# Two chained transformer blocks on one core: loads, copies, first groups and adaLN sums reordered, and one GpSimd subtraction of 1024 columns per weight unit

## The chip, the cores and the metric

The kernel runs on one core of a Trainium2 chip. The metric is device time in microseconds (us) of one execution of the whole program. The weights stream from HBM; no input is resident.

## The reference

Two blocks follow each other on 256 tokens of width 1024, all in fp32. The first is a two-layer decoder, the second a two-layer network whose layers are modulated by an adaLN vector. Cut to what matters:

```
# first block, for l in 0, 1
h = rmsnorm(x, g_mix_pre[l]);  parts = split(h @ w_in[l])          # 1024 x 1952
mix = concat(diff_attention, mla_attention, swa_attention) @ w_out[l]
x = x + rmsnorm(mix, g_mix_post[l])
xo = softmax(q(x) @ k(mem)) @ v(mem) @ w_xo[l]                      # w_xq, w_xkv, w_xo
x = x + rmsnorm(xo, g_x_post[l])
gate, up = split(rmsnorm(x, g_ffn_pre[l]) @ w_ffn_in[l])            # 1024 x 5632
x = x + rmsnorm((silu(gate) * up) @ w_ffn_out[l], g_ffn_post[l])    # 2816 x 1024
# second block: mod = silu(c) @ ada_w + ada_b gives shift, scale, gate (9 vectors a layer);
# y = swiglu_ffn(x * (1 + scale) + shift); x = layer_norm(ALPHA * x + res * gate * y)
# context and x pass a half-step FFN; layer 0: FFN, neighbourhood attention, FFN;
# layer 1: FFN, short convolution (sc_w_in, sc_conv, sc_w_out), FFN
```

## The kernel before

**Tiling.** The 256 tokens are two tiles of 128 (`t` = 0, 1). Every big product keeps the activations (128x128 pieces, transposed) as TensorE's stationary operand and streams weights as the moving one. Weights arrive in 654 units of 128x1024 fp32 through a ring of four slots. A product in fp32 accuracy is made of three matmuls on fp32r operands: `w_hi*h_hi`, `w_lo*h_hi`, `w_hi*h_lo` (L2138 to L2140). So a unit passes four engines: SyncE (SP) issues its DMA into `land` (L621) when the slot's last low half is made; ScalarE (ACT) rounds it to `w_hi` (L892, `split`) when TensorE has used the slot's last unit; GpSimd (POOL) makes `w_lo = land - w_hi` (L787, `lo`), in two operations of 512 columns; TensorE (PE) runs 12 matmuls of 512 columns on it.

**Groups.** A group is four units: the whole contraction of 1024 for 512 output columns. `group` (L2149 on) goes by unit: both token tiles of a unit, 12 matmuls, then the next unit. `group_by_tile` goes through all four units for tile 0 (6 matmuls each), then again for tile 1; it frees the first slot only after 30 matmuls. It opens the products whose input `h` is still being made. `first_group(width, aside)` is the first group of an FFN or of the K and V product of the neighbourhood attention; with `aside` (set at two places: the first FFN of layer 0 of the second block, and that K and V product) the input `h` was made earlier, and the output goes to banks TURN and OUT.

**FFN.** `ffn_in` is 11 groups, `ffn_out` 22 units, each with four parts (2 tiles x 2 halves of 512 columns, 3 matmuls a part). The last four units are taken apart: tile 0's halves first, so that the norm of tile 0 runs while PE does tile 1. `then` puts the making of the next `h` (transposes, L2506) ahead of these four.

**AdaLN.** The modulation (two layers of 18 groups of 512 columns) is summed beside the rest: SP loads `ada_land` in four pieces a group (`ada_begin`; a piece waits until DVE has used the last group's piece), VectorE (DVE) sums 8 steps for each vector (`ada_sums`, L2048 and L2051; two vectors in groups 0 to 9, then one) and splits the sum in high and low (L2057, L2060), PE adds over the partitions (`ada_sum`, L2739 and L2740), DVE adds the bias (`ada_rows_out`, L2071). Where PE does it inside an `ffn_out` is set by tables: after unit 7, 12 and 17 (`ADA_OUTS`), or 7 and 13 (`ADA_OUTS_2`); loads of a group start at the unit two less.

**Order.** Each engine has its own program, in program order; all of them are written from one list of stages (`forward`), and semaphores tie them. There is no scheduler. Names of stages used below: in0, mixer0, xq0, xo0, ffn_in0, ffn_out0 and the same with 1 for the first block; F200 for the context's FFN; F0a, NA, F01, F10, conv, F11 for the second.

The lines that the text refers to: L469 to L514 (`forward`), L567 to L700 (SP), L780 to L790 (`lo`), L905 to L985 (ACT at the start), L1133 on (`make_h`), L1612 (`products_q` on DVE), L2036 on (`ada_sums`), L2164 to L2204 (PE's groups), L2434 on (`ffn_out`).

## Time and profile before

| | us |
|---|---|
| median of three runs (2251.19 to 2258.12) | 2252.46 |
| the profiled execution, its own time | 2254.71 |
| its span, first to last instruction | 2252.8 |
| PE busy | 2154.2 (96%) |
| POOL busy | 1686.8 (75%) |
| ACT busy | 1070.5 (48%) |
| DVE busy | 966.1 (43%) |
| mean granted TensorE clock | 0.991 |

The profiled execution took 1.9 us more than its span, the time before the first and after the last instruction. Matmuls are pipelined, so the busy time of PE counts overlapping matmuls once, and a busy PE need not run at its full rate. L-numbers are lines of the kernel before. PEld is TensorE's weight load, POOL is GpSimd, SPq and ACTq are DMA issues of SyncE and ScalarE.

### The profile page before, as it was taken

Reading aid. Unit: us, or ns where it says so; the run is one execution under the profiler, and the core shown is the slowest. Engines: PE = TensorE matmul, PEld = TensorE weight load, DVE = VectorE, ACT = ScalarE, POOL = GpSimd, SP = SyncE. Lnnn points to the kernel's source line nnn. Section 1 sums busy time; section 2 is a strip of 40 time slices with the busy share of each in tenths; the row PEclk is TensorE's granted clock in tenths of the full one; section 3 lists DMA queues with packets and bytes.
Section 4 is the critical chain, followed back from the end, with each engine's and each line's share of the span. In section 5 each row is a group of like instructions: output and inputs, shape, how many; then the busy total and the mean of one; then the engine's idle time right before and its main releaser. Section 6 shows DMA issues by size and latency. Waiting matters only on the chain.

```text
span 2252.8 us, 32261 instructions
## 1 busy us (share of the span) xinstructions
PE 2154.2 (96%) x10197; PEld 1741.4 (77%) x10197; DVE 966.1 (43%) x1892; ACT 1070.5 (48%) x1646; POOL 1686.8 (75%) x1361
## 2 busy tenths in 40 slices
PE   8998899999988999999999999999999999999997
PEld 6787778778877787788778877887887788687886
DVE  6355676753556544544543552364111310344112
ACT  4464444445653544444454454565444544435442
POOL 5646388877544888798888879726988888697986
PEclk9999999999999999999999999999999999999999
DMA  7535387755244786687878765523656566464663
GB/s 232 165 113 163 103 296 257 261 182 166 92 138 179 260 284 255 211 300 244 296 255 284 282 218 162 187 76 113 203 179 198 166 186 207 139 222 145 193 205 120
DMA packets 135863, 447.10 MB, mean 198 GB/s; under 512 B 22539, under 2 KB 28131, under 8 KB 135769
## 3 DMA queue, kind: packets, MB, share of 16 engines
q1 hardware_dynamic: 129080, 426.62, 57.4%
q10 hardware_dynamic: 6688, 19.23, 2.5%
q8 instruction: 58, 0.95, 0.2%
q14 instruction: 37, 0.30, 0.0%
HBM read 444.60 MB, written 3.03 MB: 199 GB/s over the span
## 4 chain that ended last, share of the span: by engine, by line
POOL 49%; issue 29%; PE 20%; DVE 1%; POOLq 1%; ACT 0%; DMA 0%; SPq 0%; ACTq 0%; DVEq 0%
POOL w_lo L787 48%; PE ps L2138 5%; PE ps L2140 5%; PE ps L2139 5%; PE ps L2647 1%; PE ps L2612 1%; PE ps L2635 1%; PE ps L2475 1%; POOLq L187 0%; PE ps L2608 0%; POOL ada_land L833 0%; POOLq L785 0%; PE ps L2578 0%; PE ps L2390 0%; PE ps L2580 0%
## 5 line engine op out<-in xcount | busy, mean ns | idle before, releaser
L787 POOL TENSOR_TENSOR w_lo<-land,w_hi 128x512 fp32r<-128x512 f32 x1300 | 1650.3, 1303 | 518.0 <-ACT w_hi L892 516.9
L892 ACT ACTIVATE w_hi<-land 128x1024 fp32r<-128x1024 f32 x654 | 692.5, 1061 | 942.4 <-PE ps L2140 736.9
L2138 PE MATMUL ps<-w_hi,h_hi 128*128 128x512 f32 (+1 forms) x1840 | 734.6, 399 | 52.8 <-POOL w_lo L787 24.4
L2140 PE MATMUL ps<-w_hi,h_lo 128*128 128x512 f32 (+1 forms) x1840 | 720.6, 392 | 0.0
L2139 PE MATMUL ps<-w_lo,h_hi 128*128 128x512 f32 (+1 forms) x1840 | 719.5, 391 | 0.0
L2138 PEld LDWEIGHTS ps<-w_hi,h_hi 128*128 128x128 f32 x1840 | 348.0, 189 | 150.1 <-POOL w_lo L787 39.6
L2140 PEld LDWEIGHTS ps<-w_hi,h_lo 128*128 128x128 f32 x1840 | 347.8, 189 | 74.0
L2139 PEld LDWEIGHTS ps<-w_lo,h_hi 128*128 128x128 f32 x1840 | 348.4, 189 | 67.3
L1530 DVE TENSOR_TENSOR hid_lo<-ps,hid_hi 128x512 f32 (+1 forms) x77 | 53.2, 691 | 550.5 <-ACT hid_hi L1044 550.5
L2138 PE MATMUL ps<-w_hi,hid_hi 128*128 128x512 f32 x616 | 245.2, 398 | 5.7 <-POOL w_lo L787 5.7
L2140 PE MATMUL ps<-w_hi,hid_lo 128*128 128x512 f32 x616 | 243.5, 395 | 0.0
L2139 PE MATMUL ps<-w_lo,hid_hi 128*128 128x512 f32 x616 | 243.4, 395 | 0.0
L2051 DVE SCALAR_TENSOR_TENSOR ps<-ada_land,ccol,ps 128x512 f32<-128x512 f32 x322 | 230.5, 750 | 20.6 <-DMA ada_land<-ada_w_dram 12.6
L2138 PEld LDWEIGHTS ps<-w_hi,hid_hi 128*128 128x128 f32 x616 | 115.7, 188 | 36.5 <-POOL w_lo L787 7.9
L2140 PEld LDWEIGHTS ps<-w_hi,hid_lo 128*128 128x128 f32 x616 | 115.7, 188 | 28.0
L2139 PEld LDWEIGHTS ps<-w_lo,hid_hi 128*128 128x128 f32 x616 | 115.8, 188 | 27.0
L1128 ACT ACTIVATE h_hi<-ps 128x512 fp32r<-128x512 f32 x56 | 33.0, 597 | 61.6 <-DVE ps L1479 33.1
L2138 PE MATMUL ps<-w_hi,m_hi 128*128 128x512 f32 x128 | 53.6, 418 | 5.1 <-POOL w_lo L787 3.6
L1647 DVE TENSOR_TENSOR hid<-ps,sg 128x256 f32<-128x256 f32 x110 | 41.1, 415 | 37.8 <-ACT sg L1038 37.8
L1727 DVE SCALAR_TENSOR_TENSOR ps<-ps,rows 128x512 f32<-128x512 f32 x24 | 15.9, 693 | 93.2 <-PE ps L2140 93.2
L2140 PE MATMUL ps<-w_hi,m_lo 128*128 128x512 f32 x128 | 51.2, 400 | 0.0
L2139 PE MATMUL ps<-w_lo,m_hi 128*128 128x512 f32 x128 | 51.2, 400 | 0.0
(276 smaller groups left out, 1911.4 us busy)
## 6 DMA issues: line engine op xcount, KB each, us to landing
land<-ffn_w_in_dram SPq DMA_DIRECT2D x220, 512.0 KB, 3.6
ada_land<-ada_w_dram SPq DMA_DIRECT2D x144, 512.0 KB, 5.2
land<-ffn_w_out_dram SPq DMA_DIRECT2D x110, 512.0 KB, 4.1
land<-w_ffn_in_dram SPq DMA_DIRECT2D x88, 512.0 KB, 3.9
land<-w_ffn_out_dram SPq DMA_DIRECT2D x44, 512.0 KB, 4.1
land<-na_w_qkv_dram SPq DMA_DIRECT2D x40, 512.0 KB, 4.2
land<-w_xkv_dram SPq DMA_DIRECT2D x32, 512.0 KB, 3.6
land<-w_in_dram SPq DMA_DIRECT2D x32, 488.0 KB, 3.5
```

What stands on the lines that cost most here:

```text
L787: done = pool.tensor_tensor(w_lo[:, slot, half], land[:, slot, half], w_hi[:, slot, half].bitcast(F32), ALU.subtract)
L892: act.activation(w_hi[:, slot, :], land[:, slot, :], ACT.Copy).then_inc(*my.up("hi_ready"))
L1128: act.activation(half_of(h_hi, i), turned_bank(i), ACT.Copy).then_inc(*my.up("split_hi"))
L1530: dve.tensor_tensor(lo_dst, bank(TURN + kp).rearrange("p (a b) -> p a b", a=2), hi_src.bitcast(F32), ALU.subtract).then_inc(*my.up("split_ ...
L1647: ins_ = dve.tensor_tensor(hid[:, g % 2, t, :], got, sg[:, t, :], ALU.mult)
L2051: ins_ = dve.scalar_tensor_tensor(acc, w, c, acc, ALU.mult, ALU.add)
L2138: pe.matmul(dst, lh, wh, start=first, stop=False)
L2139: pe.matmul(dst, lh, wl, start=False, stop=False)
L2140: done = pe.matmul(dst, ll, wh, start=False, stop=last)
L2475: done = pe.transpose(ps[0:m, b, c * SEQ + t * P:c * SEQ + (t + 1) * P], tile, ident[:, :])
L2612: yield pe.matmul(s[:, t * SEQ:(t + 1) * SEQ], q[:, t * P:(t + 1) * P], k, start=(c == 0), stop=(c == len(mp["qk"]) - 1))
L2635: done = pe.transpose(ps[:, TURN + m % 2, at * P:(at + 1) * P], e[:, j * P:(j + 1) * P], ident[:, :])
```

## The change

1. **POOL.** The low half of a unit is one operation of 1024 columns in place of two of 512.
2. **Start.** The eight small tables (`load_constants`) are issued by SP behind the first four weight units, no longer by ACT; ACT makes the first high half of `h` ahead of the first unit's, issues the load of `mem` last, and splits `tables` in two: it rounds four units, squares `mem` (`square_memory`), rounds one unit, runs `tables`, rounds three.
3. **K and V weights of layer 0.** The seven DMAs that shift the position bias in DRAM stand behind units 7 to 13 of this stream instead of ahead of it.
4. **`aside` groups** go by unit (`group`) and not by tile.
5. **Last four units of `ffn_out`.** Tile 0's parts go in the order of `LAST_FOUR`: both halves of units 0 and 1, the first halves of 2 and 3, the second halves of 2 and 3.
6. **AdaLN.** In `ffn_out` PE adds after units 8, 13, 17 (ffn_out0), 8, 13 (ffn_out1) or 8, 12, 16 (F200, F0a), and loads start three units before. In `products_q` DVE makes four of the eight steps, copies out the first half of the queries, and then makes the rest. In `products_y` the second product's sum is added on PE one unit later, and the second of two loads starts at unit 5, its last steps behind the last unit.

```diff
-ADA_OUTS, ADA_OUTS_2, COLUMNS_AT = (7, 12, 17), (7, 13), 9
+ADA_OUTS, ADA_OUTS_2, ADA_OUTS_3, COLUMNS_AT = (8, 13, 17), (8, 13), (8, 12, 16), 9
...
+LAST_FOUR = ((0, 0), (0, 1), (1, 0), (1, 1), (2, 0), (3, 0), (2, 1), (3, 1))
...
+RPB_AT = 7
...
-            do("ffn_out", "ffn_w_out_200", ada=ADA_OUTS, then=dict(src="x", mod=(0, 0)))
+            do("ffn_out", "ffn_w_out_200", ada=ADA_OUTS_3, then=dict(src="x", mod=(0, 0)))
...
+            def products_in(l):
+                stream(f"w_in{l}", 0, 16, None if l else {RING - 1: load_constants})
...
             def kv_weights(w):
                 if n_kv[0] == 0:
-                    for j in range(7):
-                        src = bass.AP(ins["na_rpb_2"].tensor, (4 + j) * RPB_W + 15,
-                                      [(RPB_H * RPB_W, NA_H), (-1, GRID), (1, GRID)])
-                        sp.dma_start(rpb_w[:, :, j, :], src).then_inc(sems["rpb_out"], 16)
-                stream(w, 0, KV_UNITS)
+                    stream(w, 0, KV_UNITS, {RPB_AT + j: lambda j=j: shifted_rpb(j) for j in range(7)}, rolled=False)
+                else:
+                    stream(w, 0, KV_UNITS)
...
-                extra = ada_extra([3] if keys else [0, 3][0:sums])
+                extra = ada_extra([3] if keys else [0, 5][0:sums])
+                if sums > 1:
+                    late = [extra.pop(at) for at in (8, 9)]
+                    extra[7] = lambda steps=[extra[7], *late]: [step() for step in steps]
...
-                extra = ada_extra([at - 2 for at in ada])
+                extra = ada_extra([at - 3 for at in ada])
...
-                for half in (slice(0, UW // 2), slice(UW // 2, UW)):
-                    done = pool.tensor_tensor(w_lo[:, slot, half], land[:, slot, half], w_hi[:, slot, half].bitcast(F32), ALU.subtract)
-                done.then_inc(*my.up("lo_ready"))
+                pool.tensor_tensor(w_lo[:, slot, :], land[:, slot, :], w_hi[:, slot, :].bitcast(F32), ALU.subtract).then_inc(*my.up("lo_ready"))
...
                 if l == 0:
+                    split(RING)
+                    square_memory()
+                    split(1)
+                    tables()
                     split(RING - 1)
-                    tables()
-                    split(RING + 1)
...
                 if now:
+                    high(0)
                     split(1)
-                    high(0)
                     high(1)
                     split(RING - 1)
-                    load_constants()
                     high(2)
                     high(3)
+                    load_io("mem")
                     return
...
             def products_q(w):
                 dve.wait_ge(*my.last())
-                ada_sums()
+                ada_steps(range(0, KC // 2))
                 scaled_out("q_x", 0, GW, 0, R_X, "taken")
-                dve.wait_ge(*my.last())
+                ada_sums(range(KC // 2, KC))
                 ada_rows_out()
...
-                group_by_tile((TURN, OUT) if aside else (0, 2), width, fresh=True, aside=aside)
-                if aside:
+                if not aside:
+                    group_by_tile((0, 2), width, fresh=True)
+                else:
+                    pe.wait_ge(sems["split_lo"], my.at("split_lo", n["split_lo"]))
+                    group((TURN, OUT), width)
...
                 if sums:
-                    after[2] = ada_sum
+                    after[3] = ada_sum
...
-                for half in range(2):
-                    for j in range(4):
-                        if half == 0:
-                            pe.wait_ge(sems["lo_ready"], my.at("lo_ready", u + j + 1))
-                        done = part(u + j, FC - 4 + j, {0: (half,)})
-                    done.then_inc(*my.up("y_ready"))
+                for j, half in LAST_FOUR:
+                    if half == 0:
+                        pe.wait_ge(sems["lo_ready"], my.at("lo_ready", u + j + 1))
+                    done = part(u + j, FC - 4 + j, {0: (half,)})
+                    if j == 3:
+                        done.then_inc(*my.up("y_ready"))
```

Two places of the order, before and after the change (line numbers of the change are higher by 14 to 26).

ScalarE in in0, from the fifth weight unit on. Before: `L892` rounds a unit, `L927` squares `mem`, `L929` to `L933` are the tables.

```order
L892 ACTIVATE w_hi<-land 128x1024 [waits w_used,landed2]
L927 ACTIVATE z,stat<-io 128x1024 [waits io_in,squares]
L927 ACTIVATE z,stat<-io 128x1024
L929 ACTIVATE csig<-ccol 128x16 [waits start_in]
L931 ACTIVATE lam<-lam 128x4 [waits start_v]
L932 ACT_TABLE_LOAD
L932 ACTIVATE cosb<-ang 128x32
L933 ACTIVATE sinb<-ang 128x32
L892 ACTIVATE w_hi<-land 128x1024 [waits w_used,landed3]
```

Now:

```order
L918 ACTIVATE w_hi<-land 128x1024 [waits w_used,landed3]
L937 ACTIVATE z,stat<-io 128x1024 [waits io_in,squares]
L937 ACTIVATE z,stat<-io 128x1024
L918 ACTIVATE w_hi<-land 128x1024 [waits w_used,landed0]
L941 ACTIVATE csig<-ccol 128x16 [waits start_in]
L943 ACTIVATE lam<-lam 128x4 [waits start_v]
L944 ACT_TABLE_LOAD
L944 ACTIVATE cosb<-ang 128x32
L945 ACTIVATE sinb<-ang 128x32
L918 ACTIVATE w_hi<-land 128x1024 [waits w_used,landed1]
```

Two units (the eighth in slot 3 and the ninth in slot 0) moved ahead of the tables.

VectorE in xq0, between the row statistics of x and the attention: the adaLN steps and the copies of the queries (`tok_x`). Before:

```order
L2048 TENSOR_SCALAR ps<-ada_land,ccol 128x512 x2
L2051 SCALAR_TENSOR_TENSOR ps<-ada_land,ccol,ps 128x512 x14
L2057 CAST ada_hi<-ps 128x512 x2
L2060 TENSOR_TENSOR ada_lo<-ps,ada_hi 128x512 x2
L1556 TENSOR_SCALAR tok_x<-ps,stat 128x512 x2
L2071 TENSOR_TENSOR ada_o<-ps,ada_b 2x512
L1556 TENSOR_SCALAR tok_x<-ps,stat 128x512 x2
```

Now:

```order
L2061 TENSOR_SCALAR ps<-ada_land,ccol 128x512 x2
L2064 SCALAR_TENSOR_TENSOR ps<-ada_land,ccol,ps 128x512 x6
L1570 TENSOR_SCALAR tok_x<-ps,stat 128x512 x2
L2064 SCALAR_TENSOR_TENSOR ps<-ada_land,ccol,ps 128x512 x8
L2076 CAST ada_hi<-ps 128x512 x2
L2079 TENSOR_TENSOR ada_lo<-ps,ada_hi 128x512 x2
L2090 TENSOR_TENSOR ada_o<-ps,ada_b 2x512
L1570 TENSOR_SCALAR tok_x<-ps,stat 128x512 x2
```

The first copy of the queries moved ahead of eight steps and of the split of the sum, which now stand behind it.

## Rows read from the trace of the kernel before

**Rows 1.** The page: busy time, share of the span and instructions of each engine.

```profile
PE 2154.2 (96%) x10197; PEld 1741.4 (77%) x10197; DVE 966.1 (43%) x1892; ACT 1070.5 (48%) x1646; POOL 1686.8 (75%) x1361
```

**Rows 2.** Waits by pair: engine, line, waited for: total us, times, longest.

```profile
PEld ps L2138 <- POOL w_lo L787: 51.8, 51, 5.1
```

**Rows 3.** Timeline in F200: start us, us, engine, operation [idle before].

```profile
1001.50 0.39 PE L2138 MATMUL ps<-w_hi,h_hi 128*128 128x512 f32 x1
1001.73 0.39 PE L2139 MATMUL ps<-w_lo,h_hi 128*128 128x512 f32 x1
...
1002.16 2.55 POOL L787 TENSOR_TENSOR w_lo<-land,w_hi 128x512 fp32r<-128x512 f32 x2 [0.17 <-ACT w_hi L892]
```

**Rows 4.** POOL: groups by form; and timeline, eight operations behind each other.

```profile
L855 POOL TENSOR_TENSOR x<-z,rows 128x1024 f32<-128x1024 f32 x1 | 2.3, 2347 | 10.0 <-ACT z L1233 10.0
...
932.04 10.00 POOL L787 TENSOR_TENSOR w_lo<-land,w_hi 128x512 fp32r<-128x512 f32 x8 [6.46 <-ACT w_hi L892]
```

**Rows 5.** Timeline of PE at the last four units of F01.

```profile
1732.77 0.50 PE L2138 MATMUL ps<-w_hi,hid_hi 128*128 128x512 f32 x1 [1.69 <-POOL w_lo L787]
```

**Rows 6.** Timeline of PE, sixth unit of F10 behind a layer norm.

```profile
1771.29 0.50 PE L2138 MATMUL ps<-w_hi,h_hi 128*128 128x512 f32 x1 [0.46 <-POOL w_lo L787]
```

**Rows 7.** Timeline of PE and ACT, first group of F0a.

```profile
1133.98 0.50 PE L2138 MATMUL ps<-w_hi,h_hi 128*128 128x512 f32 x1 [1.24 <-POOL w_lo L787]
...
1138.94 0.49 PE L2138 MATMUL ps<-w_hi,h_hi 128*128 128x512 f32 x1 [0.81 <-POOL w_lo L787]
...
1138.95 1.21 ACT L1209 ACTIVATE z<-ps,stat 128x1024 f32<-128x1024 f32 x1
```

**Rows 8.** Timeline of SP and ACT at the K and V product of NA.

```profile
1319.20 15.88 SPq L723 DMA_DIRECT2D ada_land<-rpb_w  x24
1335.44 14.32 SPq L621 DMA_DIRECT2D land<-na_w_qkv_dram  x7
...
1339.59 1.06 ACT L892 ACTIVATE w_hi<-land 128x1024 fp32r<-128x1024 f32 x1 [2.30 <-DMA land<-na_w_qkv_dram]
```

**Rows 9.** Timeline of PE, waits at the adaLN sums of ffn_out0, ffn_out1 and F200.

```profile
437.09 0.40 PE L2739 MATMUL ps<-ada_hi,pick_r 128*2 128x512 f32 x1 [1.22 <-DVE ada_lo L2060]
...
892.55 0.39 PE L2739 MATMUL ps<-ada_hi,pick_r 128*2 128x512 f32 x1 [1.08 <-DVE ada_lo L2060]
...
1118.21 1.94 PE L2506 MATMUL ps<-ident,x 128*128 128x128 f32 x16 [1.07 <-DVE ada_o L2071]
```

**Rows 10.** Timeline of DVE, two ends of sums in ffn_out0.

```profile
438.22 0.68 DVE L2071 TENSOR_TENSOR ada_o<-ps,ada_b 2x512 f32<-2x512 f32 x1 [1.18 <-PE ps L2740]
...
453.32 0.68 DVE L2071 TENSOR_TENSOR ada_o<-ps,ada_b 2x512 f32<-2x512 f32 x1 [1.18 <-PE ps L2740]
```

**Rows 11.** Timeline of DVE and PE in xq0.

```profile
213.85 9.31 DVE L2051 SCALAR_TENSOR_TENSOR ps<-ada_land,ccol,ps 128x512 f32<-128x512 f32 x14
225.72 1.40 DVE L1556 TENSOR_SCALAR tok_x<-ps,stat 128x512 f32<-128x512 f32 x2
...
227.17 1.97 PE L2475 MATMUL ps<-ident,tok_x 128*128 128x128 f32 x8 [4.93 <-DVE tok_x L1556]
...
233.97 2.32 PE L2612 MATMUL ps<-keysT,qT_x 128*128 128x256 f32 x10
```

**Rows 12.** Timeline of PE at the start, and a stretch with its clock: us, PE busy (x), PEclk, DMA share, GB/s.

```profile
37.99 0.78 PE L2138 MATMUL ps<-w_hi,h_hi 128*128 128x488 f32 x1 [4.65 <-POOL w_lo L787]
...
38.00:42.50 4.50, 4.50 (x11) 0.50 0.58 148
```

**Rows 13.** Timeline of DVE in in0 (distances), and the group of L1805 by form.

```profile
40.56 2.60 DVE L1441 TENSOR_SCALAR dist<-pos_r,pos_c 128x256 f32<-128x256 f32 x2
...
L1805 DVE TENSOR_TENSOR ps<-z,rows 128x1024 f32<-128x1024 f32 x10 | 20.7, 2066 | 0.7
```

**Rows 14.** Timeline of ACT and PE: first K and V unit of layer 0.

```profile
67.27 1.06 ACT L892 ACTIVATE w_hi<-land 128x1024 fp32r<-128x1024 f32 x1 [9.96 <-DMA land<-w_xkv_dram]
...
70.94 0.50 PE L2138 MATMUL ps<-w_hi,m_hi 128*128 128x512 f32 x1 [3.60 <-POOL w_lo L787]
```

More of the change, by code:

```diff
@@ L489, in forward @@
                 ln_rows(i, 0, 2, 0)
-                do("ffn_out", f"ffn_w_out_2{i}0", ada=ADA_OUTS if i == 0 else (), then=dict(src="z", folded=0) if i == 0 else None)
+                do("ffn_out", f"ffn_w_out_2{i}0", ada=ADA_OUTS_3 if i == 0 else (), then=dict(src="z", folded=0) if i == 0 else None)
                 do("ln", "x", 0.5, FC, folded=None if i == 0 else 4)
@@ L765, in _ @@
             forward({
-                "start": start, "products": products, "products_conv": products_conv, "products_in": lambda l: stream(f"w_in{l}", 0, 16), "kv_weights": kv_weights,
+                "start": start, "products": products, "products_conv": products_conv, "products_in": products_in, "kv_weights": kv_weights,
                 "products_q": lambda w: stream(w, 0, 8), "products_na": lambda: stream("na_w_qkv", 0, 4 * NA_GROUPS), "products_y": products_y, "ffn_in": ffn_in, "ffn_out": ffn_out,
@@ L905, in split, with square_memory @@
                     unit()
[L907 to L923 removed]
+            def square_memory():
                 act.wait_ge(sems["squares"], my.at("squares", n["squares"]))
@@ L927, in tables @@
                     act.activation(z[:, t, :], io[:, t, :], ACT.Square, accum_out=stat[:, 28 + t:29 + t]).then_inc(*my.up("squares"))
+            def tables():
                 act.wait_ge(sems["start_in"], my.next("start_in", 16 * START_LOADS))
@@ L2034, in products_conv, with ada_steps @@
                 evict(5)
-            def ada_sums():
-                g = ada_at[0]
-                both = ada_vectors(g)
-                for k in range(KC):
+            def ada_steps(ks):
+                both = ada_vectors(ada_at[0])
+                for k in ks:
                     if k % 2 == 0:
@@ L2052, in ada_sums @@
                         ins_.then_inc(*my.up("ada_steps"))
+            def ada_sums(ks=range(KC)):
+                g = ada_at[0]
+                both = ada_vectors(g)
+                ada_steps(ks)
                 if g > 0:
@@ L2162, in group, with group_by_tile @@
                         after[j]()
-            def group_by_tile(banks, width, fresh=False, after=None, aside=False, left=(h_hi, h_lo)):
+            def group_by_tile(banks, width, fresh=False, after=None, left=(h_hi, h_lo)):
                 u = n["units"]
@@ L2169, in group_by_tile @@
                 for t in range(T):
-                    if fresh and not aside:
+                    if fresh:
                         name, value = free[t]
```

34 lines of the change are left out of this document (18 added, 16 removed).

## The prediction

> **What bounds the kernel now.** I read the page first: PE is busy for 96% of the span and the next engine, POOL, for 75% [rows 1]. In F200's steady state POOL's pair of operations takes 2.55 us and then waits 0.17 us for ScalarE, a cycle of 2.72 us; PE starts its 512-column matmuls 0.23 us apart, and 12 of them fill that same cycle [rows 3]. So PE sets the pace and POOL stands just under it, at 94%. 654 units of 2.72 us are 1779 us that no part of this change touches: its matmuls are the same. What can go is time in which PE waits. The waits by pair put 51.8 us in 51 waits on `w_lo` [rows 2], and the timelines of PE show the rest one by one, on adaLN sums and on copies. A matmul shown behind an idle stretch began about 0.17 us later than the idle says (the row gives the one before it 0.39 us, but the next could start after 0.23), so a wait costs its idle plus 0.17.
>
> **POOL's operation.** The trace has POOL operations of 1024 columns: 2.35 us [rows 4]. Against a pair at 2.55 us on time that is 0.20 less before a low half is ready; eight pairs behind each other take 10.00 us for four units, 2.50 each [rows 4], so in a backlog a unit gains 0.15. Steady stretches gain nothing, PE hides it; when PE's sequence is behind a norm, POOL works through a backlog and PE waits a little at each unit, as at F10's sixth unit, 0.46 + 0.17 [rows 6]. Such waits over the first units of F01, F10, conv and F11 add up to 3.4 us; a backlog of four to six units at 0.15 takes off 0.5 to 0.6 at each: **2.1**. Ten places where single low halves come last (the by-tile first groups of F200 and NA, and the first units of ffn_in0, xq0, ffn_in1, xq1) at 0.12 to 0.20: **1.5**. Bounds for both: 0, if the 1024-column form costs 2.50 here, and 5.
>
> **Last four units.** In F01 PE waits 1.69 + 0.17 = 1.86 at the fourth of them [rows 5], after three parts of 0.68 us (three matmuls) each; F10 and F11 have the same wait. The new order puts two more parts ahead of it, 1.36, and POOL is 0.2 quicker at the most: the wait falls to about 0.48. 3 x 1.38 = **4.1**. Bounds: 3 and 5.6 (all of it gone).
>
> **`aside` groups.** F0a's group waits 1.24 + 0.17 and 0.81 + 0.17 at its units [rows 7], and 0.98 a third time, 3.4 in all; a unit now carries 12 matmuls before the next is needed, so these go. But ScalarE's rounding of the fifth unit stands behind the normalisation of tile 1, which ends at 1140.16 [rows 7]; rounding and low half take some 3.4 more, and a PE that is 3.4 earlier meets it: a new wait of about 1.5. **2.0**. In NA the waits were 3.4 and, on a sum, 1.2; but there SP issues 24 small bias loads over 15.88 us and only then the next weight, at 1335.44; it lands and is rounded at 1339.59 [rows 8], its low half ends at about 1343.1, while PE asked for it at 1343.4. Whatever PE gains ahead, it loses at that unit: **0**, bounds -1.5 and +1.5.
>
> **AdaLN in `ffn_out`.** PE waits for the split sum 1.22 us in ffn_out0, 1.08 in ffn_out1, and 1.07 at the transposes after it in F200 [rows 9], each + 0.17. One unit more (2.72) covers all three: 1.25 in ffn_out1, 1.23 in F200. In ffn_out0 DVE's sums are a chain: two sums end 15.1 us apart [rows 10], and three groups at 8, 13, 17 now leave 9 units, 24.5 us, between the first and the third, for 30.2 us of chain, less what the earlier load gives. The first wait goes (1.39), the third comes in with 2 us or so: **-0.5**, bounds -3 and +1.4. Sum of the three: **2.0**.
>
> **xq0 and xq1.** Fourteen of the sixteen steps take 9.31 us, 0.665 each, and PE's transposes wait 4.93 + 0.17 for the first copy of the queries behind them and the split [rows 11]. With eight steps (5.3) and the split (2.6) moved behind it, the copy is 7.9 earlier and the transposes start at 222.1, when PE is free. DVE does the same operations in another order, so its last one, now the split of the sum instead of the copy, still ends at 227.1. PE, which has done a unit by then (2.7 and the transposes), waits for it some 1.5, adds it up in four matmuls (0.9) and starts the scores at about 228.3, where it did at 233.97 [rows 11]; the stretch at half clock behind the 4.93 us idle is gone with it. **5.7**, bounds 3 (if the new idle brings the half clock too) and 6.4 (no new wait). xq1 has no such wait: 0.
>
> **xo0 and xo1.** PE's waits on the sums go, but DVE's own chain (steps, split, new x) sets when x is ready. I take one wait of the size of ffn_out1's [rows 9] for both together: **1.3**, bounds 0 and 4 (three such).
>
> **Start.** The position bias no longer stands ahead of the K and V weights: ScalarE's 9.96 us wait for the first of them becomes short, and PE's 3.60 + 0.17 goes [rows 14], with a half-clock stretch behind it (1.4): 5.2. In in0 two units are rounded ahead of the tables, and PE's wait of 4.65 + 0.17, which was followed by 4.5 us at a granted clock of 0.50 [rows 12], and another of 0.8 on `h_lo` could go too, in all 9. Against this stands DVE. [...] With POOL's at 2.35 us, each `dist` in lockstep takes 2.35: eight of them, 10.4 us before, take 18.8, and DVE's tile of the queries comes at about 55.4 where PE wants it at 49.8. This takes the 9 back: in0 gets -1.7 in my sum. Start: **3.5**, bounds 0 and 14.
>
> [...]
>
> **Sum.** 2.1 + 1.5 + 4.1 + 2.0 + 0 + 2.0 + 5.7 + 1.3 + 3.5 = 22.2 us. The profiled execution took 2254.7 us, 1.9 beyond its span, and was 2.2 above the median; from it 2254.7 - 22.2 = 2232.5, and by the median 2252.46 - 22.2 = **2230**.
>
> **The rivals.**
>
> *The start keeps its gain* (0.17). DVE's operations there don't stretch with POOL's: then 9 + 5.2 at the start, and 1 more elsewhere, sum 33 and about 2220. For it: it is not shown that a wider POOL operation is one block; against: `dist`'s time equals POOL's operation, not its own size.
>
> *Blocking spreads* (0.15). The mixer's softmax and xq0 also have such DVE operations beside POOL; 16 of them at 0.6 us more, on a path on which PE waits, cost up to 10, and the start and xq0 lose 2. Gain 10: about 2242. For it: same engines, same buffers; against: POOL is idle in much of the mixers, since weights are rounded ahead only as far as the ring of four.
>
> *The change doesn't do what it says* (0.05): one operation of 1024 costs the pair's 2.50. Then 2.1 + 1.5 and part of the last-four term are lost, 4.2: about 2234. The 2.35 us of two other forms [rows 4] speak against it.
>
> *Slower* (0.03). [...]
>
> **How the numbers follow.** The forecast has 0.60, with its own range from 2224 to 2238 by the bounds of its terms (not all fall on one side). 0.3% is 6.8 us, about what a measurement of this kernel can tell from no change; the boundary is 2245.7. The range 2216 to 2244 takes in the first three rivals and leaves out the tails and the slower one. Faster 0.92; within 0.3% 0.06 (the far end of the spreading rival); slower 0.02.
>
> **What would show it.** In the profile after: `w_lo` x650 at 2.35 us mean; F01, F10, F11 with under 0.6 us of wait in the last four; no waits inside F0a's first group, but one at its fifth unit; NA's same unit at the same distance from SP's last bias load; PE's transposes of `tok_x` without a wait, the scores 5.7 us earlier; no 9.96 us wait of ScalarE at the first K and V unit; `dist` at 2.35 us and PE waiting for `scaled_out`'s tile near 50 us. The prediction is wrong if `dist` stays at 1.3, if mixers grow by more than 1 us each, or if steady stretches of `ffn_in` no longer run at 2.72 us per unit, since everything rests on PE's pace being untouched.

## The result, and the profile after it

The changed kernel took 2231.86 us, median of 4 runs (2229.97 to 2238.67), beside 2255.29 us for the kernel before in the same comparison: a ratio of 0.9899, 95% interval 0.9865 to 0.9933. The prediction was 2230 (2216 to 2244). The profiled execution took 2231.26 us, its span 2229.5, against 2254.71 and 2252.8 before.

The total came out within 2 us of the forecast, but several terms did not come out: errors of opposite sign hid each other. So the total is no test of the terms; the stretches of PE are.

First the page of the changed kernel, which answers to [rows 1], and its costliest group on POOL:

```profile
PE 2145.7 (96%) x10197; PEld 1743.3 (78%) x10197; DVE 988.1 (44%) x1892; ACT 1070.1 (48%) x1646; POOL 1594.6 (72%) x711
...
L814 POOL TENSOR_TENSOR w_lo<-land,w_hi 128x1024 fp32r<-128x1024 f32 x650 | 1558.1, 2413 | 580.8 <-ACT w_hi L918 578.2
```

650 operations of 2.41 us stand for 1300 of 1.30; in steady state one takes 2.40, in a backlog they start 2.36 apart. DVE has the same 1892 instructions and is busy 22 us longer. The waits on `w_lo` by pair answer to [rows 2], 51.8 us in 51:

```profile
PEld ps L2157 <- POOL w_lo L814: 13.3, 18, 1.7
PE ps L2157 <- POOL w_lo L814: 13.3, 14, 5.5
```

The table gives the length of stretches of PE, in us, from one stage's first matmul to the next's, worked out from the starts in each trace. The program is the same in a column and the "again" beside it: the kernel before and the changed one were each profiled twice (the second executions are experiments 11 and 12). "Wide alone" is experiment 2, "narrow" experiment 1.

| stretch | before | again | wide alone | narrow | changed | again |
|---|---|---|---|---|---|---|
| in0 | 69.50 | 66.53 | 63.72 | 60.52 | 61.18 | 67.15 |
| K/V and mixer, layer 0 | 95.64 | 95.43 | 96.03 | 93.76 | 95.15 | 95.06 |
| K/V and mixer, layer 1 | 93.03 | 92.58 | 94.33 | 93.19 | 95.92 | 95.52 |
| xq0 | 52.04 | 51.81 | 51.55 | 47.92 | 47.42 | 46.93 |
| xo0 | 28.82 | 28.81 | 28.78 | 28.35 | 28.35 | 28.37 |
| xo1 | 34.04 | 34.15 | 33.22 | 32.02 | 32.02 | 32.00 |
| ffn_out0 | 70.28 | 70.28 | 70.14 | 70.79 | 70.79 | 70.80 |
| F200, ffn_out | 66.41 | 66.40 | 66.41 | 65.14 | 65.14 | 65.14 |
| F0a, ffn_in | 130.71 | 130.72 | 130.15 | 128.38 | 128.25 | 128.23 |
| F0a, ffn_out | 66.40 | 66.40 | 66.41 | 65.14 | 65.14 | 65.14 |
| NA, K and V product | 51.39 | 51.09 | 50.29 | 54.83 | 53.35 | 52.92 |
| NA, the rest | 139.86 | 141.40 | 140.74 | 139.85 | 145.53 | 139.13 |
| F10, ffn_in | 128.73 | 128.71 | 127.38 | 128.70 | 127.36 | 127.38 |
| F10, ffn_out | 70.01 | 70.00 | 69.87 | 68.65 | 68.51 | 68.50 |

The F rows, xo0 and ffn_out0 repeat within 0.1 us from one execution of a program to the next; the mixers, xq0, xo1 and NA's K and V product within 0.5. In0 and NA's rest do not: the second execution of the changed kernel took 6 us more in one and 6 us less in the other, and the sum of all stretches hardly moved, 2215.48 and 2216.11. Some stretches that are not in the table vary too: ffn_in1 took 128.97 and 130.39 us in the changed kernel (the second had 3.1 us at half clock, a granted clock of 0.50), and in the kernel before layer 1's w_in took 49.00 and 47.89 and xq1 45.23 and 46.09.

The places that the prediction named, on PE of the changed kernel. The fourth of the last four units: no stall in F01, F10 or F11 above 0.4 us, where [rows 5] showed 1.69; the row below is F11's. F0a's fifth unit; NA's fifth unit; the third sum of ffn_out0; the sum in xq0, and the scores behind it:

```profile
2209.35 0.50 PE L2157 MATMUL ps<-w_hi,hid_hi 128*128 128x512 f32 x1 [0.20 <-POOL w_lo L814]
...
1124.51 0.50 PE L2157 MATMUL ps<-w_hi,h_hi 128*128 128x512 f32 x1 [1.29 <-POOL w_lo L814]
...
1322.07 0.76 PE L2157 MATMUL ps<-w_hi,h_hi 128*128 128x512 f32 x1 [5.51 <-POOL w_lo L814]
...
454.91 0.39 PE L2761 MATMUL ps<-ada_hi,pick_r 128*2 128x512 f32 x1 [2.82 <-DVE ada_lo L2079]
...
218.58 0.40 PE L2761 MATMUL ps<-ada_hi,pick_r 128*2 128x512 f32 x1 [1.37 <-DVE ada_lo L2079]
219.50 2.75 PE L2634 MATMUL ps<-keysT,qT_x 128*128 128x256 f32 x12
```

Each wait is where the prediction put it: 0.2 + 0.17 (0.48 forecast), 1.5 (1.5), 5.7 (3.4 + 1.2 = 4.6, what PE was to gain ahead of it), 3.0 (2 or so), 1.5 (1.5).

### The profile page after: what moved, and what is told of

It is laid out like the page before. It is cut to its first block, busy times and chain, and to the rows that moved or that the text cites. A ratio compares the mean times of both kernels' runs of the same rounds, so it can differ in the third digit from the quotient of the medians.

```text
span 2229.5 us, 31551 instructions
## 1 busy us (share of the span) xinstructions
PE 2145.7 (96%) x10197; PEld 1743.3 (78%) x10197; DVE 988.1 (44%) x1892; ACT 1070.1 (48%) x1646; POOL 1594.6 (72%) x711
## 4 chain that ended last, share of the span: by engine, by line
PE 35%; POOL 30%; issue 27%; DVE 7%; ACT 1%; POOLq 1%; DMA 0%; SPq 0%; DVEq 0%; ACTq 0%
POOL w_lo L814 29%; PE ps L2157 9%; PE ps L2159 9%; PE ps L2158 9%; PE ps L2669 2%; DVE ps L2064 1%; PE ps L2657 1%; PE ps L2634 1%; PE ps L2497 1%; PE ps L2630 0%; PE ps L2412 0%; POOLq L191 0%; DVE h_lo L1502 0%; POOL ada_land L859 0%; POOLq L813 0%
## 5 line engine op out<-in xcount | busy, mean ns | idle before, releaser
L814 POOL TENSOR_TENSOR w_lo<-land,w_hi 128x1024 fp32r<-128x1024 f32 x650 | 1558.1, 2413 | 580.8 <-ACT w_hi L918 578.2
```

What stands on the lines that cost most here:

```text
L814: pool.tensor_tensor(w_lo[:, slot, :], land[:, slot, :], w_hi[:, slot, :].bitcast(F32), ALU.subtract).then_inc(*my.up("lo_ready"))
```

## The experiments

Times are spans and medians as given by each run; the verdicts rest on stretches of PE, since one execution of this kernel differs from the next by several us. Where a run has one execution only, the text says so. In the short diffs `-` is the changed kernel unless said otherwise.

### 1. Narrow: two operations again

```diff
-                pool.tensor_tensor(w_lo[:, slot, :], land[:, slot, :], ...)
+                for half in (slice(0, UW // 2), slice(UW // 2, UW)):
+                    done = pool.tensor_tensor(w_lo[:, slot, half], land[:, slot, half], ...)
```

> The change with POOL's one operation of 1024 columns put back to two of 512; everything else as changed. Theory A (the wide operation ends a low half 0.15 to 0.2 us sooner, but blocks an operation of DVE on the shared path for its whole length, as L1877 in mixer0, 0.27 us before and 1.21 after): in each of the two mixers PE's waits behind the probabilities go back from 1.64 and 2.71 to 0.89 and 1.77, 1.7 us a layer, 3.4 in all; at the start DVE's operations on the angles (2.33 us each) halve and PE's 3.83 us wait for zin falls under 1, 4 us; the latencies give back 3.6 to 4. Net 3 to 5 us shorter than the change, 2225 to 2229. Theory B (the wide operation costs DVE nothing that reaches PE): mixers and start unchanged, 3.6 us longer than the change, 2235.

2231.9 us median of 4, ratio to before 0.9887 (0.9857 to 0.9917): no difference from the change that the medians can show. In the stretches A holds for the mixers, 1.4 and 2.7 us shorter, and for the low halves, 1.3 us longer in F10's and F11's ffn_in, 0.6 in F01's, conv's and F200's. It fails for the start: in0 changed by 0.7, not 4. The gain and the price of the wide operation stand in different places. Over the stretches from F200 on, NA's attention left out, the wide operation is 7.0 us shorter by the two profiles; the mixers cost 3.4 by their waits (below). A net gain of 3 or 4 us is less than the intervals of the two medians can tell from nothing.

### 2. Wide alone, in the kernel before

```diff
 (kernel before)
-                for half in (slice(0, UW // 2), slice(UW // 2, UW)):
-                    done = pool.tensor_tensor(w_lo[:, slot, half], land[:, slot, half], ...)
-                done.then_inc(*my.up("lo_ready"))
+                pool.tensor_tensor(w_lo[:, slot, :], land[:, slot, :], ...).then_inc(*my.up("lo_ready"))
```

> The kernel before with the one operation of 1024 columns alone. Theory A: 3.6 us gained at the low halves (last four of ffn_out: each wait 1.86 to about 1.65; by-tile groups 0.12 to 0.2 each; sixth units of F10, conv, F11 0.3 each), 3.4 us lost in the mixers, and a loss of some us in in0, where eight DVE operations go from 1.3 to 2.35 each; net 0 to 8 us longer than before. Theory B: 3.6 us shorter than before, no stretch longer.

2246.09 us median of 10, ratio 0.9955 (0.9934 to 0.9975): faster by about 10 us (5.6 to 14.9), more than either theory said, and more than its stretches that repeat show. Those behind norms gave 4.4 us: F01 0.70, F10 1.35, conv 0.59, its second product 0.36, F11 1.39. The mixer of layer 1 lost 1.3 (1.8 against the second execution of before). In0, which I had expected to lose, was 63.72, less than in either execution of before. The cause is not the low half alone: PE did not wait for the first K and V unit there, which it does in both executions of before (3.77 and 3.6 us).

### 3. NA's first group by tile again

```diff
-                    pe.wait_ge(sems["split_lo"], my.at("split_lo", n["split_lo"]))
-                    group((TURN, OUT), width)
+                    n_aside.append(1)
+                    if len(n_aside) == 2:
+                        group_by_tile((TURN, OUT), width, fresh=True, aside=True)
+                    else:
...
```

> The change, but the first group of NA's K and V product goes by tile again. Theory A (SP's 24 bias loads ahead of the fifth unit set when that unit comes, whatever PE gained ahead, and an idle of 5.7 us brings a stretch of PE at half clock that a row of short waits does not): the wait of 5.67 at unit 380 falls to under 1.5, short waits of 0.8 to 1.2 come back at the first three half units, no half clock, and the K and V stretch (53.35 us in the change, 51.39 before) comes out near 51: 2 us shorter. Rival: the stretch depends on the unit alone, so 53.3 again. Whether the half clock in NA's attention (1455 to 1463, 5.5 us lost) comes back is open: it is the same code and the same waits as before.

The K and V product took 51.84 us (53.35 and 52.92 in the change): A, with 1.1 to 1.5 us. The wait at the fifth unit was 1.8, the short waits were 1.25, 0.85 and 0.86. No part of this stretch ran at half clock; 6.8 us of it did in both executions of the change. So the change by unit costs at this place: PE, which is 3.4 us earlier, meets SP's bias loads in one long idle (5.5 us in the change's first profile), and the granted clock is 0.50 for 6.8 us around its end. 2 us had been expected. The median of four was 2229.17 (2222.91 to 2234.54), ratio 0.9878 (0.9841 to 0.9915).

### 4. NA's bias loads spread

```diff
-                for h in range(NA_BIAS):
-                    load_bias(h)
+                for h in range(NA_BIAS):
+                    for r in range(4):
+                        spread_out.append(lambda h=h, r=r: bias_part(h, r))
```

and `stream` issues two of the list behind each unit, from the fifth on.

> The change, with NA's 24 bias loads issued two behind each weight unit of the K and V product from the fifth on, not all ahead of the fifth. Theory A: the 5.67 us wait at unit 380 and the half clock behind it go and the K and V stretch falls from 53.35 to about 45.5, total 7 us shorter than the change, 2224. Rival (the fifth unit is late for another cause, ScalarE's normalisation as in F0a): the wait stays at 1.5 or more, 4 us shorter at most.

47.92 us: 5.2 less than the mean of the change's two. The wait fell from 5.7 to 1.56 and the granted clock was 1.00 all through the stretch. 7 us had been expected, with the stretch near 45.5. What is left at that unit is the rival's cause, as in F0a: ScalarE rounds the unit (from 1318.10 us on) directly behind its normalisation of tile 1. The median was 2225.67 (2222.62 to 2230.55), ratio 0.987 (0.9838 to 0.9903). The change leaves this gain unused.

### 5. Position bias ahead of the K and V weights again

```diff
-                    stream(w, 0, KV_UNITS, {RPB_AT + j: lambda j=j: shifted_rpb(j) for j in range(7)}, rolled=False)
+                    for j in range(7):
+                        shifted_rpb(j)
+                    stream(w, 0, KV_UNITS)
```

> The change, with the seven shifts of the position bias issued ahead of the K and V weights of layer 0 again. Prediction's term: 5.2 us lost (PE idle 3.77 at the first K and V unit and a half-clock stretch). Rival, from the run of the wide operation alone, where the first K and V unit landed 5.9 us after its issue, not 9.4 as before, and PE did not wait: the term depends on how fast these small transfers land in one execution, and PE, which gets to that unit at 62 us and not at 67, waits 2 to 9 us.

In0 61.37 us (61.18) and the stretch behind it 96.79 (95.15): 1.8 us in all, and no wait of PE at the first K and V unit. This is one execution (2233.06 us); in experiment 4, which has the change's code in both stretches, they took 61.27 and 96.09, and beside that it is 0.8. ScalarE waited there, though less than the 9.96 us of [rows 14]:

```profile
59.22 1.06 ACT L920 ACTIVATE w_hi<-land 128x1024 fp32r<-128x1024 f32 x1 [6.31 <-DMA land<-w_xkv_dram]
```

SP issued the seven shifts from 44.38 us on, 5.3 us earlier than before, and PE came to the unit at 62.8, when its low half was just ready. Neither the 5.2 us of my term nor the rival's wait of 2 to 9 us came. The 5.2 was the price in the kernel before; with SP running ahead in the changed kernel, the same DMAs cost 0.8 to 1.8.

### 6. ScalarE's old order in in0

```diff
-                    split(RING)
-                    square_memory()
-                    split(1)
-                    tables()
-                    split(RING - 1)
+                    split(RING - 1)
+                    square_memory()
+                    tables()
+                    split(RING + 1)
```

> The change, with ScalarE's old order in in0 (three units, squares of mem and the tables together, five units). Theory A: the eighth and ninth units' high halves come after the squares and the tables, which now wait for SP's eight tables, and PE's idle at unit 7 comes back: 4 to 5 us, of which 3.8 were at unit 8 for zin in the change, so in0 grows by 1 to 4 us from 61.2 (with a half clock, at the upper end). Rival: mem's load, now last on ScalarE's queue, is there in time and nothing is lost: in0 stays within 0.5 us.

In0 60.86 us, 0.3 less, where 1 to 4 more had been expected: the wait at unit 7 came back (3.14) and the one at unit 8 (3.83) went. One queue or the other makes PE wait about as long there. Rounding two units earlier gave nothing in this one execution (2227.76 us).

### 7. First copy of the queries behind the sum again

```diff
-                ada_steps(range(0, KC // 2))
-                scaled_out("q_x", 0, GW, 0, R_X, "taken")
-                ada_sums(range(KC // 2, KC))
+                ada_sums()
+                scaled_out("q_x", 0, GW, 0, R_X, "taken")
+                dve.wait_ge(*my.last())
```

> The change, with the first copy of xq0's and xq1's queries behind all sixteen steps and the split again. Theory: PE's 5.1 us wait at unit 47 comes back and the waits of 1.53 on the sum and 2.12 behind the second copy go; with the half clock xq0 is 4 to 5 us longer than 47.42, xq1 within 1 us.

Xq0 took 52.07 us, as before (52.04), against 47.42 and 46.93: this edit is worth 4.9 us by itself (one execution, 2238.02 us). Xq1 took 44.49 (44.52). PE's wait is the one of [rows 11] again:

```profile
224.20 1.97 PE L2497 MATMUL ps<-ident,tok_x 128*128 128x128 f32 x8 [4.98 <-DVE tok_x L1570]
```

The change has another wait there, which the prediction did not have: 1.96 us of idle ahead of the scores of tile 1. It is a block like those of experiment 8. Behind the first scores DVE has an operation of two columns, and the operations of the changed kernel, DVE's and POOL's, are:

```profile
222.33 2.03 DVE L1881 TENSOR_SCALAR mstat<-mstat 128x2 f32<-128x2 f32 x1
```

```profile
221.98 2.35 POOL L814 TENSOR_TENSOR w_lo<-land,w_hi 128x1024 fp32r<-128x1024 f32 x1 [2.02 <-ACT w_hi L918]
```

In experiment 6 POOL's operation came about 2 us earlier, and the block and the wait were gone; xq0 took 45.70:

```profile
221.92 0.31 DVE L1880 TENSOR_SCALAR mstat<-mstat 128x2 f32<-128x2 f32 x1
```

```profile
219.86 2.35 POOL L814 TENSOR_TENSOR w_lo<-land,w_hi 128x1024 fp32r<-128x1024 f32 x1 [0.59 <-ACT w_hi L918]
```

In the ten profiles with the changed order, this DVE operation took 0.17 to 2.13 us; in the seven in which it took 0.57 or more, PE's idle was shorter than it by 0.06 or 0.07, and in the other three it was 0.25 or less.

In this execution in0 took 66.83 us, though its code up to there is the change's (see experiment 11).

### 8. Narrow in in0 and the mixers, wide elsewhere

```diff
+                if my.narrow:
+                    for half in (slice(0, UW // 2), slice(UW // 2, UW)):
+                        done = pool.tensor_tensor(w_lo[:, slot, half], land[:, slot, half], ...)
+                    done.then_inc(*my.up("lo_ready"))
+                    return
...
+                my.narrow = my.n["units"] < 34 or 138 <= my.n["units"] < 158
```

> The change, but two operations of 512 columns for units 4 to 33 and 138 to 157 (in0, and layer 1's K and V, with the mixers), one of 1024 elsewhere. Theory A (DVE's small shared-path operations in the mixers wait for the running POOL operation to end, whatever their own size): mixer stretches as in the narrow kernel, 93.8 and 93.2 (1.4 and 2.7 shorter than the change), in0 0.5 shorter, all other stretches as in the change: 4.5 us shorter. Rival B (the mixers' difference was the clock's): no stretch differs by more than 0.5.

2218.2 us median of 4 (2217.63 to 2220.82), ratio 0.9849 (0.9813 to 0.9886). Layer 1's mixer took 92.64 us, 3 us less than the change. Not all of that is the block, for 3.4 us of the change's stretch ran at half clock and none of this one. In the profiles in which none of the stretch did, it took 94.34 with the wide operation (experiment 2) and 92.37 to 92.64 with narrow ones (the second execution of before, this one and experiment 9): 1.7 to 2.0 us. So A holds, and B accounts for the rest.

Layer 0's stretch came out no shorter (95.32, with 4.1 us at half clock against the change's 1.7). It gained at unit 28, whose wait fell to the narrow one's 0.9, but not at the last scores: my limit of 34 ended before the units that POOL subtracts behind its norm of the heads (34 and 35), where layer 1's (158) includes them. So one kernel holds both cases at that place, layer 0's with wide operations first, then layer 1's with halves:

```profile
149.43 2.08 PE L2643 MATMUL ps<-qkT 64*128 64x256 f32 x8 [2.55 <-ACT prob L1304]
...
604.02 1.13 PE L2643 MATMUL ps<-qkT 64*128 64x256 f32 x8 [1.62 <-ACT prob L1304]
```

2.55 as in the change, 1.62 as before. ScalarE's probabilities are what PE waits for; behind them is DVE. In the changed kernel's layer 0, POOL and DVE (L1877 has two columns, 0.23 us where nothing blocks it):

```profile
147.51 4.66 POOL L814 TENSOR_TENSOR w_lo<-land,w_hi 128x1024 fp32r<-128x1024 f32 x2
```

```profile
150.98 1.21 DVE L1877 TENSOR_SCALAR mstat<-mstat,sinks 128x2 f32<-128x2 f32 x1
...
153.55 0.23 DVE L1877 TENSOR_SCALAR mstat<-mstat,sinks 128x2 f32<-128x2 f32 x1
```

POOL's second operation ends at 147.51 + 4.66 = 152.17; the two-column operation that began inside it ends at 152.19. The next one, with POOL idle, takes its own 0.23.

### 9. Quarters in the mixers

```diff
+                    for part in range(my.narrow):
+                        half = slice(part * UW // my.narrow, (part + 1) * UW // my.narrow)
...
+                my.narrow = 2 if my.n["units"] < 16 else 4 if my.n["units"] < 38 or 138 <= my.n["units"] < 158 else 0
```

> The change, with two operations of 512 columns for units 4 to 15, four of 256 columns for units 16 to 37 and 138 to 157, one of 1024 elsewhere. Theory A (a DVE operation on the shared path waits for the one POOL operation that runs, so its length is that operation's): the waits in both mixers, 1.64 and 2.71 in the change, 0.89 and 1.77 with halves, go on falling, to about 0.5 and 1.3; but a unit takes POOL about 2.8 us there. Mixer stretches 0.5 to 1 us shorter than with halves (93.8, 92.6). Rival: the time from 1.64 to 0.89 came from the earlier low half alone, then quarters, whose unit is later still, make the waits longer than with halves.

Mixer stretches 93.25 and 92.37 us (halves in experiment 10: 93.36 and 93.18). The wait at unit 28, 1.64 and 0.89, fell to 0.25, as A says. The one at the last scores, 2.72 and 1.78, did not go on falling: 2.20. There one small operation, which with halves happened to begin just before the end of one of POOL's and took 0.27, now met one at its start:

```profile
144.81 0.70 DVE L1887 TENSOR_SCALAR mstat<-mstat,sinks 128x2 f32<-128x2 f32 x1
```

So the block shrinks with POOL's operation, but where a given small operation meets one is a matter of phase. The stretches gained 0.1 and 0.8 on the halves, where 0.5 to 1 had been expected. Of the 0.8, about 0.6 is the clock: the halves' stretch of layer 1 had 1.2 us at half clock, the quarters' none. The median of four was 2224.86 us (2218.21 to 2229.01), ratio 0.9875 (0.9852 to 0.9898).

### 10. The two gains together

Narrow for units 4 to 37 and 138 to 157 (as in experiment 8, the limit mended), and NA's bias loads spread (experiment 4).

> The change, with two operations of 512 columns for units 4 to 37 and 138 to 157 and the NA bias loads spread two to a unit: the mixers' 4.1 us and NA's K and V product's 5.4 us together, and both kernels beaten: 2215 us, 9 to 17 us below the change by what in0 and the clock happen to do; ratio to before 0.982 to 0.984. If the two gains are not additive (PE meets another wait behind them), 2221.

2218.68 us median of 5 (2213.28 to 2222.37), ratio 0.9835 (0.9813 to 0.9858). Mixers 93.36 and 93.18, K and V product 47.86: both gains are there together, 4.5 and 5.3 us by the stretches. It is faster than the kernel before by 1.65%; beside the change it is 13 us less by the medians, and its interval ends (0.9858) where the change's two begin (0.9865, and 0.9855 in experiment 11). Against experiment 8, in which in0 came out at 56.3, it is no faster (2218.2 there): in0 took 60.96 here, with the same code.

### 11. The changed kernel once more

> The changed kernel as it is, once more. If the half-clock stretch of PE in NA's attention (13.7 us long, 5.7 us lost) and the length of in0 (61.2 us) are the program's, both come back within 0.5 us. If they are one execution's, NA's 24 units and attention come out at 139 to 142 us, as in seven of the eight other kernels with the same NA code, and in0 at 56 to 67, as DVE's small operations fall before or behind POOL's first low half.

2231.91 us in the profiled execution, 2225.25 in the other, ratio 0.9886 (0.9855 to 0.9916). Neither stretch came back: in0 67.15, NA's rest 139.13. In NA the waits are the same in both, the same 1.68 us before the same product, but not the clock. The windows of PE over the same 14 us of NA's attention, which stands 7 us later in the second profile (us, PE busy (x), PEclk, DMA share, GB/s), first profile and then second:

```profile
1453.00:1467.00 14.00, 14.00 (x65) 0.51 0.16 42
```

```profile
1460.00:1474.00 14.00, 14.00 (x118) 1.00 0.27 68
```

In0 is the better find. PE, first profile and second, at the thirteenth unit, waiting for DVE's copy of tile 1:

```profile
51.47 0.48 PE L2157 MATMUL ps<-w_hi,h_hi 128*128 128x488 f32 x1 [0.41 <-DVE zin L1570]
```

```profile
55.50 0.78 PE L2157 MATMUL ps<-w_hi,h_hi 128*128 128x488 f32 x1 [5.80 <-DVE zin L1570]
```

DVE ahead of that copy. First profile:

```profile
43.50 0.18 DVE L1474 TENSOR_TENSOR ccol<-ccol,csig 128x16 f32<-128x16 f32 x1
43.72 0.62 DVE L1455 TENSOR_SCALAR dist<-pos_r,pos_c 128x256 f32<-128x256 f32 x2
44.37 2.85 DVE L1457 SCALAR_TENSOR_TENSOR dist<-dist 128x512 f32<-128x512 f32 x1
47.25 2.77 DVE L1458 TENSOR_TENSOR dist_w<-dist,band 128x512 f32<-128x512 f32 x1
50.06 1.36 DVE L1570 TENSOR_SCALAR zin<-ps,stat 128x488 f32<-128x488 f32 x2
```

Second profile:

```profile
43.67 2.12 DVE L1474 TENSOR_TENSOR ccol<-ccol,csig 128x16 f32<-128x16 f32 x1
45.82 2.70 DVE L1455 TENSOR_SCALAR dist<-pos_r,pos_c 128x256 f32<-128x256 f32 x2
48.56 2.75 DVE L1457 SCALAR_TENSOR_TENSOR dist<-dist 128x512 f32<-128x512 f32 x1
51.34 2.71 DVE L1458 TENSOR_TENSOR dist_w<-dist,band 128x512 f32<-128x512 f32 x1
54.09 1.36 DVE L1570 TENSOR_SCALAR zin<-ps,stat 128x488 f32<-128x488 f32 x2
```

And POOL, first and second:

```profile
36.10 7.05 POOL L814 TENSOR_TENSOR w_lo<-land,w_hi 128x1024 fp32r<-128x1024 f32 x3 [4.51 <-ACT w_hi L918]
44.27 2.40 POOL L814 TENSOR_TENSOR w_lo<-land,w_hi 128x1024 fp32r<-128x1024 f32 x1 [1.11 <-ACT w_hi L918]
```

```profile
36.23 14.52 POOL L814 TENSOR_TENSOR w_lo<-land,w_hi 128x1024 fp32r<-128x1024 f32 x6 [3.61 <-ACT w_hi L918]
```

In the first, POOL had a pause of 1.11 us from 43.15 on, and three DVE operations ran in it at their own length, 0.18 and 0.31 each. In the second POOL had six low halves without a pause, and each of those operations but one lasted until one ended. The difference is 4 us on DVE, 5.4 in PE's wait, and 6 with the clock behind it, which was 0.50 for 6.8 us from 53.0 on.

### 12. The kernel before once more

No edit.

> The kernel before as it is, once more. In its first profile the first K and V unit landed 9.4 us after its issue behind the seven shifts of the position bias and PE waited 3.77 us; with the wide operation alone it landed after 5.9 us and PE did not wait. If that wait is the program's, it comes back within 1 us. If it is one execution's, in0 (69.5 us to the first K and V matmul) is 64 to 67 here. All stretches behind the mixer of layer 0 should be the same within 0.2 us but for half-clock stretches of 1.7 us each.

2250.89 us, one execution. The wait at the first K and V unit came back, 3.6 us, so it is no accident of the first profile; experiment 2, which has the same order of loads, did not have it. In0 was 3 us shorter all the same, 1.7 of it because the half clock at the 4.6 us wait lasted 3.4 us and not 6.8. NA's rest had 3.4 us at half clock, which the first profile had not. The stretches behind norms repeat within 0.05. Xq1 (0.9 longer) and ffn_out1 (0.5) did not keep to the 0.2 that was expected, and neither had any time at half clock.

## Why the prediction was right, and where it was not

**Last four units: right.** 1.36 a place against 1.38, and 0.14 from the wide operation. One place of three gave less. In F11 the end is not PE's: DVE's chain of the final norm starts with the first half of tile 0, which follows the last low half at once in either order, before and in the change:

```profile
2233.16 0.70 DVE L1775 SCALAR_TENSOR_TENSOR ps<-ps,rows 128x512 f32<-128x512 f32 x1 [44.94 <-PE ps L2140]
```

```profile
2210.43 0.70 DVE L1789 SCALAR_TENSOR_TENSOR ps<-ps,rows 128x512 f32<-128x512 f32 x1 [44.84 <-PE ps L2159]
```

From there to the end of the span it is 19.7 and 19.0 us. PE's stretch to its last matmul is 1.5 us shorter, the rest after it 0.8 longer. I had added the three places as if each ended in a matmul.

**Low half: right in kind, mis-sized.** After norms 2.1 was forecast, 4.4 measured. I gave a backlog of four to six units 0.15 each. A unit in a backlog takes 2.36 against 2.50, 0.14 less, and yet the waits of 0.42 and 0.63 at the seventh and eighth unit of F10 are both gone (the second is the one of [rows 6], which is the eighth unit and not the sixth). The by-tile places, 1.5 forecast for ten, gave more too: the wide operation alone (experiment 2, both executions of before beside it) took 0.6 from F200's ffn_in, 0.5 from ffn_in0, 0.3 to 0.5 from xq0 and 0.8 to 1.1 from NA's K and V product.

**`aside`: F0a right, NA wrong by 1.9.** F0a's ffn_in gained 2.5, of which 0.6 by the wide operation (2.0 forecast for the edit; 1.9 measured on top of the wide operation, 2.3 without it). In NA the step "whatever PE gains ahead, it loses at that unit: 0" left out what it loses besides: with one idle of 5.5 us instead of three short ones the granted clock is 0.50 for 6.8 us, 4.7 of them with PE busy. The K and V product got 1.9 longer, outside the bounds of 1.5 either way; experiment 3, by tile, takes 1.1 to 1.5 of it back. The sum's wait that I had booked there as a set-off belongs to F0a's ffn_out, and it went, 1.26, like F200's.

**AdaLN in `ffn_out`: right.** 1.2, 1.3 and -0.5, each as forecast, with the third sum 3.0 us late in ffn_out0.

**xq0: right in mechanism, 0.6 to 1.1 less.** 4.9 by experiment 7, 4.6 to 5.1 by the stretches, for 5.7. The sum's wait was 1.54 as forecast; the step that failed is that nothing else waits. The scores of tile 1 wait (1.96 + 0.17), because DVE's two-column operation behind the first scores is blocked by POOL (experiment 7). Where it was not, with no part of the stretch at half clock (experiments 6 and 9), xq0 took 45.70, a gain of 6.1 to 6.3. So the term depends on when POOL's operation falls. Xo0 and xo1 gave 0.5 and 2.0, for 1.3 forecast for both; before, 3.4 us of xo1 ran at half clock, which the change's first profile did not have.

**Start: the term failed, both ways.** It said 3.5, of 5.2 for the bias shifts and -1.7 for in0. The 5.2 is what a wait cost in the kernel before; in the changed kernel undoing the edit costs 0.8 to 1.8. The -1.7 does not follow from the figures beside it either: 9 gained and a wait of 5.6 leave 3.4, less what the clock takes; and the figures shown for the 9 add up to 7.9 (4.82, half of 4.5, and 0.8). For in0 I took all of DVE's small operations as blocked, one after the other, and so its copy at 55.4. No run shows the term that my sum has for them, eight operations in 18.8 us: from the first of the eight to the end of the last it was 10.5 us in the kernel before, 13.3 in the first profile of the change and 17.2 in the second. What I took for certain is one of two things that happen: the copy ended at 51.4 in the first profile and 55.4 in the second, and PE waited 0.57 and 5.97, for a forecast of 5.6. What I had not seen is that in a pause of POOL's these operations take their own time, 0.18 and 0.31 us where they took 2.12 and 2.44 beside it (experiment 11). Nor had I seen a wait that both profiles have, 3.8 and 3.0 us ahead of the ninth unit, where PE wants DVE's copy for the transposes of `mem`. Which DVE operations meet POOL goes with small shifts. In the six profiles with the change's code in in0, POOL's first low half started between 19.68 and 20.22 us in the four with an in0 of 61.2 to 61.4, and at 20.46 and 20.70 in the two with 66.8 and 67.2. With halves it is the other way round: 19.89 and 20.34 for an in0 of 60.5 and 61.0 (experiments 1 and 10), 20.74 and 20.95 for 56.3 and 56.5 (experiments 8 and 9), with the same code at the start. No run moved that start by itself, so that it decides is argued and not shown.

**Mixers: the rival I gave 0.15 did happen in part.** "Blocking spreads" priced the mixers at up to 10; it was 3.4 by the waits (1.64 for 0.89 and 2.71 for 1.77, in each layer), and my sum had 0. In layer 1 it is visible in the stretch, 2.9 longer, of which 1.7 to 2.0 is the block and the rest the clock (experiment 8). In layer 0 it is hidden: there the kernel before had 6.4 us at half clock, 3.4 of them behind its wait for the first K and V unit, and the changed one 1.7. By the prediction's own sign of being wrong, mixers more than 1 us longer, this part was wrong in layer 1, and by the waits in both; and `dist`, which was to be at 2.35, took 0.31 in the first profile (experiment 11). The rival's step held in xq0 as well. In experiments 8, 9 and 11 a small DVE operation that began beside one of POOL's ended within 0.05 us after it: 1.21 for an operation of 0.23, 2.12 for one of 0.18, and 0.70 for one of 0.23 when POOL's take 0.72. What the same runs show besides is that the cost goes by the time that POOL is busy, not by the number of DVE's operations: a pause of 1.11 us let three of them through at their own length.

**What the total hides.** Low halves behind norms 2.3 us better than forecast, xo0 and xo1 1.2; mixers 3.4 worse, NA's K and V 1.9, xq0 0.8, F11's end 0.8; and in0, between 4.8 better and 1.1 worse, with NA's clock from 5.7 worse to nothing, in whichever execution was profiled. In each of the two profiles of the change one of those two went wrong and the other did not, so that both came to the same time. That the total agreed with the forecast within 2 us is luck.

What stays open: why the clock falls in NA's attention in some executions and not in others. The waits ahead of it are the same to 0.01 us (1.68 and 0.41), and it fell to 0.50 in seven of the fourteen profiles (twelve experiments, and one of each kernel before them), for 13.7 us once, for 6.8 twice and for 3.4 four times. No run changed it at will.

## What to carry to other kernels

When an operation is widened on an engine beside which small operations of another last until it ends, as DVE's did beside POOL here (1.21 us for 0.23), its gain stands where that engine works through a backlog (2.36 us a unit for 2.50), and its price at those small operations of the other engine that are on the path: put the wide form where the first holds and the narrow where the second does (experiments 8 and 10). Before pricing a chain of blocked operations, look for the pauses of the blocker: they, not the count, say how many are blocked. And compare stretches that repeat; a total that comes out right can be two errors.

## What was not expected of the hardware

A DVE operation of two columns took 1.21 us beside POOL and 0.23 without, which the mean of its group (0.36 over 16) hides; another took up to 2.13 and 0.17 without, and PE waited for it (experiment 7). Operations with a single small input were blocked as well; two of the changed kernel's in in0, 32 columns each, 0.18 us where POOL pauses:

```profile
22.14 2.33 DVE L1441 TENSOR_SCALAR ang<-ang 128x32 f32<-128x32 f32 x1
24.51 2.34 DVE L1442 TENSOR_SCALAR ang<-ang 128x32 f32<-128x32 f32 x1
```

Two executions of one program differ by 6 us in in0 and by 6.4 in NA's rest, while most stretches between repeat within 0.1. And at the idle before the fifth unit of NA's K and V product the granted clock was 0.50 for 6.8 us, from 0.8 to 3.6 us before PE started again, in all eight profiles in which that idle was over 5 us, and in none of the six in which it was under 2.
